# Inner layer norms: variance summed by token quarters on the column tiles, root and reciprocal on 66 columns

## The reference

```
def _standardize(x):
    mu = jnp.mean(xf, -1, keepdims=True)
    var = jnp.mean(jnp.square(xf - mu), -1, keepdims=True)
    return (xf - mu) * lax.rsqrt(var + LN_EPS)
...
x = layer_norm(ALPHA * x + (1 + gate) * m, ln_g, ln_b)     # after each sublayer
h = x * (1 + scale) + shift                                # adaLN input of the next one
```

## Time and profile before

| | before |
|---|---|
| median of 3 runs | 837.84 us (837.76 to 838.95) |
| the profiled execution | 836.97 us |
| its span | 835.1 us |
| mean granted TensorE clock | 0.947 |
| PE / PEld busy | 736.1 us (88%) / 467.2 us |
| DVE / ACT / POOL busy | 243.6 / 276.7 / 126.8 us |
| HBM over the span | 338 GB/s |

### The profile page before, as it was taken

One profiled execution on the slowest core, in us unless ns is written; L12 is line 12 of the kernel. 1 busy time (PEld: TensorE's weight loads), 2 busy tenths in 40 slices (PEclk: granted clock), 3 DMA queues, 4 the chain that ended last, 5 costly groups with the idle time before them and its releaser, 6 DMA issues.

```text
span 835.1 us, 22462 instructions
## 1 busy us (share of the span) xinstructions
PE 736.1 (88%) x9570; PEld 467.2 (56%) x9571; DVE 243.6 (29%) x603; ACT 276.7 (33%) x555; POOL 126.8 (15%) x211
## 2 busy tenths in 40 slices
PE   3799999899999999988786789978999979979992
PEld 2477887576556656554443348735656535546651
DVE  1138998813810100000000273165100000000007
ACT  1134677511423333323222142033333313323330
POOL 0170687500010101000000000000101001000100
PEclk9999999699999999999899779999999989999996
DMA  9999522894994999999999999699699999999901
GB/s 308 391 235 379 212 101 102 315 369 173 407 416 167 379 382 373 422 416 428 417 425 423 391 361 397 263 386 368 273 382 428 416 425 425 415 428 417 411 4 52
DMA packets 64237, 281.53 MB, mean 337 GB/s; under 512 B 2989, under 2 KB 3603, under 8 KB 55990
## 3 DMA queue, kind: packets, MB, share of 16 engines
q1 hardware_dynamic: 61474, 273.88, 83.2%
q0 software_dynamic: 2048, 5.86, 2.3%
q10 hardware_dynamic: 676, 1.24, 0.5%
HBM read 278.54 MB, written 3.37 MB: 338 GB/s over the span
## 4 chain that ended last, share of the span: by engine, by line
PE 59%; DMA 25%; DVE 8%; SPq 3%; ACT 2%; issue 2%; POOL 0%; DVEq 0%; ACTq 0%
PE bank L746 17%; DMA ring<-in_w_up 14%; PE bank L756 8%; PE bank L1025 7%; PE bank L887 7%; PE bank L719 5%; PE bank L785 5%; DMA ring<-in_w_in_even 4%; DMA big<-in_w_up 4%; DVE t L1382 3%; DMA ring<-in_w_ada 2%; PE bank L587 2%; DMA big<-in_state_pool 2%; DVE big L1376 2%; SPq L483 2%
## 5 line engine op out<-in xcount | busy, mean ns | idle before, releaser
L746 PE MATMUL bank<-ring,big 128*32 128x256 f32 x2112 | 130.7, 403 | 30.8 <-DMA ring<-in_w_up 27.3
L746 PEld LDWEIGHTS bank<-ring,big 128*32 128x32 f32 x2112 | 73.3, 116 | 84.1 <-DMA ring<-in_w_up 25.4
L1839 DVE SCALAR_TENSOR_TENSOR big<-big,bank 128x128 f32<-128x128 f32 x49 | 17.0, 347 | 318.8 <-ACT big L1318 318.8
L1970 POOL TENSOR_TENSOR big<-t 128x192 f32<-128x192 f32 x51 | 26.4, 518 | 542.8 <-PE bank L719 405.9
L719 PE MATMUL bank<-htm,big 128*32 128x256 f32 x1224 | 75.6, 379 | 1.2 <-POOL big L1973 1.2
L887 PE MATMUL bank<-big,ring 128*128 128x264 f32 x320 | 74.1, 390 | 0.8 <-DMA ring<-in_w_in_even 0.8
L746 PE MATMUL bank<-big 128*32 128x256 f32 x1024 | 63.5, 404 | 11.5 <-DMA big<-in_w_up 8.1
L887 PEld LDWEIGHTS bank<-big,ring 128*128 128x128 f32 x320 | 60.0, 190 | 12.5 <-issue 2.0
L756 PE MATMUL bank<-ring,big 128*32 128x256 f32 x1056 | 63.8, 382 | 0.0
L1318 ACT ACT_TABLE_LOAD x49 | 62.9, 1283 | 1.7 <-issue 0.9
L1318 ACT ACTIVATE big<-bank 128x128 f32<-128x128 f32 x49 | 13.6, 277 | 148.3 <-PE bank L746 148.3
(11 more groups left out here) (261 smaller groups left out, 810.9 us busy)
## 6 DMA issues: line engine op xcount, KB each, us to landing
ring<-in_w_ada SPq DMA_DIRECT2D x24, 2048.0 KB, 18.5
ring<-in_w_gate SPq DMA_DIRECT2D x21, 2048.0 KB, 22.3
ring<-in_w_up SPq DMA_DIRECT2D x21, 2048.0 KB, 25.2
ring<-in_w_down SPq DMA_DIRECT2D x21, 2048.0 KB, 26.3
big<-in_w_gate SPq DMA_DIRECT2D x11, 2048.0 KB, 14.8
big<-in_w_up SPq DMA_DIRECT2D x11, 2048.0 KB, 18.8
big<-in_w_down SPq DMA_DIRECT2D x11, 2048.0 KB, 19.5
ring<-in_w_in_even SPq DMA_DIRECT2D x5, 2048.0 KB, 31.1
```

Of the source, the lines that this page charges most:

```text
L746: last = mm(GU[C * q:C * (q + 1), :].rearrange("p (a n) -> p a n", a=2), hgc[:, P * (k % 2) + C * (k // 2):P * (k % 2) + C * (k // 2 + 1)] ...
L1970: v.tensor_tensor(flat, all_r, all_b[:, :, bass.ds(g, 1)].broadcast_to([P, 2 * TT, C]), ALU.mult)\
```

## The change

The squares of all eight tiles are now summed by token quarters: for each tile, four products of 66 tokens (`T // 4`) each go to the four column tiles, so that each group of 32 partitions holds the full sum over features of its own quarter of the tokens, in 66 columns. There is nothing left to add across groups, so ScalarE takes the root of 66 columns straight from `VAR_PART` (scale `1.0 / D`), and VectorE the reciprocal of 66 columns. VectorE then multiplies it with a mask `quadrant` (1 where a partition group meets its own quarter, 0 elsewhere), which lays the four quarters side by side in `ln_part`, 264 columns wide. The spread product, at its old place in TensorE's queue, then puts the reciprocal on all partitions, and the tiles of `t1` are multiplied by that bank, divided by 32 (`1.0 / C`). The mask is filled once at the start by five memsets.

```diff
+        quadrant = sb("quadrant", [P, 4, T // 4])
...
             def layer_norm_var(idx):
-                for half in range(2):
-                    pe.wait_ge(E("ln_sq"), 4 * idx + 2 * half + 2)
-                    last = partial_sums(VAR_PART[idx], t2, range(4 * half, 4 * half + 4), not half)
+                for m in range(KD):
+                    pe.wait_ge(E("ln_sq"), 4 * idx + m // 2 + 1)
+                    for q in range(4):
+                        last = mm(VAR_PART[idx][C * q:C * (q + 1), 0:T // 4], ones[:, 0:C], t2[:, m, T // 4 * q:T // 4 * (q + 1)],
+                                  start=(m == 0), stop=(m == KD - 1), tile_position=(0, C * q))
                 last.then_inc(E("ln_part_done"), 1)
...
                 act.wait_ge(E("ln_part_done"), 2 * idx + 2)
-                copy(ln_part[:, :], VAR_PART[idx], E("ln_part_copied"))
-                act.wait_ge(E("ln_var"), idx + 1)
-                A(fn(stat[:, :], LN_VAR[idx], ACT.Sqrt, scale=1.0 / (C * D), bias=epsb[:, 0:1]), E("ln_std"))
+                A(fn(stat[:, 0:T // 4], VAR_PART[idx][:, 0:T // 4], ACT.Sqrt, scale=1.0 / D, bias=epsb[:, 0:1]), E("ln_std"))
...
+            S(v.memset(quadrant[:, :, :], 0.0))
+            S.sync()
+            for q in range(4):
+                S(v.memset(quadrant[C * q:C * (q + 1), q, :], 1.0))
...
                 dve.wait_ge(E("ln_std"), idx + 1)
-                S(v.reciprocal(stat[:, :], stat[:, :]))
-                S.sync()
+                S(v.reciprocal(stat[:, 0:T // 4], stat[:, 0:T // 4]))
+                S.sync()
+                tt(ln_part.rearrange("p (q j) -> p q j", q=4), stat[:, 0:T // 4].unsqueeze(1).broadcast_to([P, 4, T // 4]), quadrant[:, :, :],
+                   ALU.mult, E("ln_part_copied"))
+                dve.wait_ge(E("ln_var"), idx + 1)
                 for p in range(4):
                     if idx == 2 and p == 2:
                         modulation()
-                    tt(t1[:, 2 * p:2 * p + 2, :], t1[:, 2 * p:2 * p + 2, :],
-                       stat[:, :].unsqueeze(1).broadcast_to([P, 2, T]), ALU.mult, E("ln_n"))
+                    stt(t1[:, 2 * p:2 * p + 2, :], LN_VAR[idx].unsqueeze(1).broadcast_to([P, 2, T]), 1.0 / C,
+                        t1[:, 2 * p:2 * p + 2, :], ALU.mult, ALU.mult, E("ln_n"))
```

## The result

The changed kernel took 842.34 us (median of 5 runs, 840.86 to 842.80), the kernel before beside it 837.84 (836.63 to 839.17): ratio 1.0049, 95% interval 1.0030 to 1.0068, so by the ratio 4.1 us slower (2.5 to 5.7). I had forecast slower, 839.7 us; the size is about twice what I gave, and it lies above my range. The profiled execution took 840.91 us with a span of 839.1 and a mean granted clock of 0.947, the same mean as before.

What follows compares the result with a forecast made beforehand. TensorE's queue behind the spread bounds the first norm, a DMA the second, VectorE the third. Terms 2.03 + 0.0 - 0.15 = +1.88 us on the median give 839.7 us, range 837.9 to 841.5.

Steps and rivals of the forecast that it cites:

- What bounds the first norm: First norm: the chain leaves at TensorE's spread product, through two adaLN units to routing, not through the reciprocal.
- the gate: First norm: the spread product, in front of TensorE's full queue, starts later and delays all behind it by 2.03 us.
- Prices on VectorE and ScalarE: Per norm: reciprocal of 66 columns 0.57 us, masked product of 264 columns 0.43, root of 66 columns 0.34.
- The variance's tail: Variance sums behind the last square: 16 records at 18.5 ns, 0.30 us; saving taken as 0.31 us.
- The second norm, 0.0: Second norm: L1065 waits for the pool state's DMA either way, so 0.0 us, bounds -0.1 and +0.3.
- The third norm, -0.15: Third norm: modulation starts at 554.00 instead of 554.15, VectorE's saved 1.3 us becoming a wait for the columns.
- both clock effects absent, or both there and cancelling: Forecast case, 839.7 us, chance 0.46: clock fall in first norm's gap and kept clock in third, both or neither.
- rival (a): Clock falls in the first norm's new gap and still in the third: +1.88 + 1.60, 841.3 us, chance 0.26.
- three gaps: TensorE idle times: 1.7 us and 2.8 us ended with the clock falling; nearly 2 us at 232.20 to 234.20 kept 1.00.

Runs made afterwards that it cites:

- the kernel with products in the gap: Changed kernel plus four products of no use between the columns and the first norm's spread, keeping TensorE busy: 839.37 us, ratio 1.0013.
- the kernel with both units ahead: Changed kernel with adaLN unit 10 ahead of the first norm's spread and unit 21 ahead of the third's: 836.84 us, ratio 0.9991.
- the last kernel: The kernel before plus six products of no use behind the second norm's spread and six behind unit 21's columns in the third: 834.77 us, ratio 0.9968.
- the three variants with the same gap: Changed kernel with unit 10 ahead of the spread (1.0002), products in the first norm's gap (1.0013), or first norm in old form (0.9983).

## Why the prediction was wrong, point by point

- **What bounds the first norm: right.** The chain goes through the spread product into the two units and routing, before and after. The forecast spread starts 2.03 us later; measured against the last square 3.29 - 1.21 = 2.08, and 2.08 again as the gate's whole cost in the kernel with products in the gap.
- **Prices on VectorE and ScalarE: right.** Reciprocal 0.56 (forecast 0.57), masked product 0.43 (0.43), root 0.32 (0.34).
- **The variance's tail: a small miss.** 16 records behind the last square took 0.44 us in the chain, the end of the last one included, and not 0.30. The next product started 0.37 us behind the first of them, so their starts lie about 23 ns apart. The least distance of about 25 ns that the Trainium skill gives (TensorE: Matmul & The Clock Gate, Part 1, "Wait — 56ns, not 53.3ns?"), which I set aside for a row of 18.5 ns, makes 0.40 us and would have been nearer, though the starts here lie a little closer than that. The miss cost 0.05 us in the first norm and 0.13 in the third, and nothing in the second.
- **The second norm, 0.0: right.** The pool state's landing still released L1068.
- **The third norm, -0.15: nearly.** Measured -0.02. L607, the columns (L606 before), came 0.77 later against the last square and not 0.64, by the same tail. The saving of 1.3 us on VectorE turned into a wait for unit 21's columns, as forecast; 0.74 us of it can be had by moving the unit, as the kernel with both units ahead shows.
- **The step that failed: the clock.** My likeliest case was "both clock effects absent, or both there and cancelling". The first was there in 5 of 5 profiles, at 1.5 us (0.54 in the spread, 0.93 in unit 10) where I had priced 1.6. The second, that the shorter idle time of about 2.0 us ahead of the third norm's routing keeps 2.4 GHz, was absent in 5 of 5. Both gaps let it fall. (Kept up by products in the gap, the clock gave 1.3 us there and not 1.60, since ScalarE's tiles then pace the twelve records.) So rival (a), 1.88 + 1.60 = 3.48 us, was the case that held; the first norm shows 3.56 us and the third -0.02, and I gave it 0.26. With the measured terms the sum is 2.08 + 1.48 - 0.02 = 3.54 us, ratio 1.0042, inside both intervals, though below both centres (4.1 and 4.7 us). The remaining 0.6 to 1.2 us is noise, or belongs to the later start of the first norm, 1.5 us in the profiles' mean; which of the two is not shown.
- **Why I leaned the wrong way.** I counted three gaps and took the one that kept the clock (232.20 to 234.20) as nearly equal evidence. There TensorE had worked without a break up to the gap and went on with a chunk of 64 records. Around the new gap stand two small products for the columns in front and a single spread behind. The two gaps that did fall had short pieces with breaks of 0.5 us in front too, though one of them had twelve full records of routing behind it. And I left out a fourth gap of the kernel before, 2.76 us ahead of L1065 in the second norm, behind which the clock fell as well. With it three of four gaps led to a fall, and (a) deserved more than 0.26. That the pieces around a gap decide was not tested, and the second norm's spread speaks against it as a rule: it too has the two products for the columns in front, and 2.14 us of idle time, and kept its clock every time.
- **Range.** It ended at 841.5, on top of rival (a). With 0.26 on that case, its own spread belonged inside.

## What to carry to other kernels

When a product moves behind a longer chain of other engines, price the whole queue behind it on its engine, and then move the work that doesn't need it ahead: one moved line was worth 3.9 us here (10.27 to 6.36), while the narrowed reciprocal had saved 1.2 us off the path. Where a wait leaves TensorE idle for 2 us or more, put a fall of the clock into the sum as a case of its own, some 1.5 us here, and measure it: of two gaps of nearly the same length, both between the columns and a spread, one ended in a fall every time and the other never. A few products of no use in such gaps held the clock, and made the otherwise unedited kernel before 0.3% faster. What such a stretch then saves reaches the end only as far as the chain stays on it: of 2.6 us in the second norm 1.3 came through.

## What the runs showed of the hardware

- Products that compute nothing of use held the granted clock: with them in the gap it stayed at 2.4 GHz (1.00 over 490.20 to 493.00 in the last kernel, 0.65 in the kernel before), and the work behind ran 1.3 to 1.7 us faster (unit 16 from 3.64 to 1.94 us, twelve routing records from 4.28 to 2.98).
- Idle times of 2.0 us (ahead of the third norm's routing) and 2.25 us (ahead of the first norm's spread) ended in a fall in 5 of 5 profiles of the changed kernel (the 2.0 us also in the three variants with the same gap, twelve records in 4.27 to 4.44 us). An idle time of 2.14 us ahead of the second norm's spread ended in none in the same five (0.71 us). Idle times of 1.4 to 2.3 us at the start of the second MoE led to a fall in five of the thirteen profiles (first chunk 5.35 us) and not in the others (3.66), and 1.94 and 2.24 us are among the others. The length of the idle time alone does not tell.
- Products of 8 columns (L1072, 16 records in 1.85 us) did not let the clock fall when full products ran before them.
- Products of 66 columns on four column tiles started about 23 ns apart behind a wait (the next product 0.37 us behind the first of 16 records), and 0.44 us passed to the end of the last.
